# Attention stage of a decoder step: where a step's scores stand on TensorE, and which bank takes the filler behind the transposes

## The reference, cut to what matters

```python
u = rms_norm(x, g_pre) @ w_in          # q: 1024 columns, z: 3 x 1024, gates
l = einsum(q, k) * scale + bias
p = masked_softmax(l, mask, -1)
o = einsum(p, v)
y = sum(gate * o * silu(z), over 3 branches)
x = x + rms_norm(y @ w_out, g_post)
```

## Time and profile before

| | |
|---|---|
| median of 3 runs | 900.47 us (899.14 to 901.45) |
| profiled execution, its own time | 900.51 us |
| its span | 898.7 us |
| TensorE (PE) busy | 867.2 us, 96% of the span |
| VectorE (DVE) busy | 557.3 us, 62% |
| ScalarE (ACT) busy | 452.9 us, 50% |
| GpSimd (POOL) busy | 300.9 us, 33% |
| TensorE in the chain that ended last | 87% of the span |

### The profile page before, as it was taken

One profiled execution on the slowest core, in us unless ns is written; L12 is line 12 of the kernel. 1 busy time (PEld: TensorE's weight loads), 2 busy tenths in 40 slices (PEclk: granted clock), 3 DMA queues, 4 the chain that ended last, 5 costly groups with the idle time before them and its releaser, 6 DMA issues.

```text
span 898.7 us, 16698 instructions
## 1 busy us (share of the span) xinstructions
PE 867.2 (96%) x6202; PEld 755.4 (84%) x6202; DVE 557.3 (62%) x1211; ACT 452.9 (50%) x916; POOL 300.9 (33%) x311
## 2 busy tenths in 40 slices
PE   5999999999999999999999999999999999999996
PEld 4999999956788788889999898999999998786664
DVE  6379999998967772423345555646464655536563
ACT  6466777634643552224446555556464555524231
POOL 2389888888140000012023232333324233400000
PEclk9999999999999999999999999999999999999999
DMA  9355433127269392446323232232232002923521
GB/s 252 97 157 161 120 103 78 54 54 230 66 226 356 139 292 63 111 78 183 95 47 72 49 71 62 58 70 62 58 72 48 24 1 53 274 88 102 184 84 36
DMA packets 158165, 99.52 MB, mean 111 GB/s; under 512 B 97202, under 2 KB 147026, under 8 KB 158005
## 3 DMA queue, kind: packets, MB, share of 16 engines
q1 hardware_dynamic: 143278, 79.30, 33.1%
q0 software_dynamic: 4896, 10.32, 3.2%
q10 hardware_dynamic: 9911, 8.84, 3.0%
HBM read 89.58 MB, written 18.85 MB: 121 GB/s over the span
## 4 chain that ended last, share of the span: by engine, by line
PE 87%; DVE 4%; ACT 3%; issue 3%; ACTq 1%; POOL 1%; DVEq 0%; POOLq 0%
PE psum L2300 8%; PE psum L2301 7%; PE psum L2302 7%; PE psum L1952 6%; PE psum L1953 6%; PE psum L1954 6%; PE psum L2395 6%; PE psum L2030 5%; PE psum L2143 4%; PE psum L2144 4%; PE psum L2145 4%; PE psum L2346 4%; PE psum L2363 3%; PE psum L1933 2%; PE psum L2328 2%
## 5 line engine op out<-in xcount | busy, mean ns | idle before, releaser
L811 ACT ACTIVATE arena<-psum 128x512 f32<-128x512 f32 (+9 forms) x227 | 90.1, 433 | 173.4 <-PE psum L2302 66.4
L2300 PE MATMUL psum<-u_hi,tile_hi 128*128 128x288 f32 x464 | 143.3, 309 | 4.5 <-ACT arena L811 2.1
L790 POOL TENSOR_SCALAR arena<-arena,kept 128x512 f32<-128x512 f32 (+3 forms) x128 | 83.1, 664 | 177.1 <-DVE kept L1789 177.1
L2301 PE MATMUL psum<-u_lo,tile_hi 128*128 128x288 f32 x464 | 137.6, 296 | 0.0
L2302 PE MATMUL psum<-u_hi,tile_lo 128*128 128x288 f32 x464 | 136.4, 294 | 0.0
L1439 DVE SCALAR_TENSOR_TENSOR psum<-arena,psum 128x512 f32<-128x512 f32 x168 | 127.0, 756 | 6.0
L1952 PE MATMUL psum<-h_hi,tile_hi 128*128 128x288 f32 x352 | 104.3, 296 | 0.0
L1953 PE MATMUL psum<-h_lo,tile_hi 128*128 128x288 f32 x352 | 103.8, 295 | 0.0
L1954 PE MATMUL psum<-h_hi,tile_lo 128*128 128x288 f32 x352 | 103.8, 295 | 0.0
L2300 PEld LDWEIGHTS psum<-u_hi,tile_hi 128*128 128x128 f32 x464 | 87.3, 188 | 10.3 <-ACT arena L811 4.0
L1261 ACT ACTIVATE arena<-arena,kept 128x512 f32<-128x512 f32 (+3 forms) x128 | 70.5, 552 | 44.7 <-DVE kept L1755 43.9
(11 more groups left out here) (328 smaller groups left out, 1898.1 us busy)
## 6 DMA issues: line engine op xcount, KB each, us to landing
tile_whole<-in_b_w_in SPq DMA_DIRECT2D x64, 256.0 KB
tile_whole<-in_a_w_in SPq DMA_DIRECT2D x24, 512.0 KB
arena<-in_cmp_w SPq DMA_DIRECT2D x4, 2048.0 KB, 9.8
kvw_whole<-in_w_kv SPq DMA_DIRECT2D x6, 1024.0 KB, 14.1
bias_copies<-bias_line POOLq DMA_DIRECT2D x4, 1280.0 KB, 23.5
arena<-in_x_prompt SPq DMA_DIRECT2D x8, 512.0 KB, 6.5
kvw_whole<-in_a_w_out SPq DMA_DIRECT2D x4, 1024.0 KB, 11.3
arena<-bias_copies SPq DMA_DIRECT2D x16, 256.0 KB, 3.8
```

Source lines behind the costliest of these rows:

```text
L790: pool.tensor_scalar(L, L, rden[:, stat(n) + k:stat(n) + k + 1], gR[:, i, h:h + 1], ALU.mult, ALU.mult).then_inc(S["pn_ready"], 1)
L811: return nc.scalar.activation(out, in_, ACT.Copy, scale=scale)
L2300: pe.matmul(pb(7, HT), w_hi, u_hi[:, k, here], start=(k == 0), stop=False)
L2301: pe.matmul(pb(7, HT), w_hi, u_lo[:, k, here], start=False, stop=False)
```

## The change

TensorE's order in a turn becomes `parts[0]`, `values(n-2)`, `scores(n)`, first transposes, `parts[1]`, second transposes. The halves that stand in `parts[1]` of steps 1, 2 and 4 no longer go to bank 7 but to the scores bank of the same step's first unit (`part_bank`). Such a half waits until VectorE has read that unit (`l_ready`), and the next step's scores wait until the half has been read out. Bank 7's own order (`own`) skips these halves. On ScalarE the read-out of `parts[0]` moves in front of the step's exponentials, and the copy of the first transposes (`pt_copy(n - 1, 0)`) moves behind the second exponential in step 3; in the last round it stood there before.

```diff
+        def in_scores_bank(n):
+            part = tile_parts(n)[1] if n % 5 in (1, 2, 4) else None
+            return part[:2] if part else None
+
+        aside = [in_scores_bank(n) for n in range(5 * KD)]
+        own = [half for half in order if half not in aside]
-        bank_clear = {half: bank_read(before) for before, half in zip(order, order[1:])}
+        bank_clear = {half: bank_read(before) for before, half in zip(own, own[1:])}
...
+        def part_bank(part, n):
+            return steps[n][3][0] % 4 if part[:2] == aside[n] else 7
...
@@ ScalarE
             for n in range(N_STEPS + 1):
+                parts = tile_parts(n)
+                drain(parts[0], n)
                 if n < N_STEPS:
...
                         for j, u in enumerate(us):
...
-                            if j == 1 and n % 5 == 1:
-                                drain(parts[0])
-                            if j == 1 and n >= LAST_PAIR:
+                            if j == 1 and (n >= LAST_PAIR or n % 5 == 3):
                                 pt_copy(n - 1, 0)
-                parts = tile_parts(n)
-                if n % 5 != 1:
-                    drain(parts[0])
-                if 1 <= n < LAST_PAIR or n == N_STEPS:
+                if 1 <= n < LAST_PAIR and n % 5 != 3 or n == N_STEPS:
                     pt_copy(n - 1, 0)
-                drain(parts[1])
+                drain(parts[1], n)
...
@@ TensorE
-            def tile_part(part):
+            def tile_part(part, n):
...
+                b = part_bank(part, n)
...
                     if k == 0:
-                        if (i, hf) in bank_clear:
+                        if b != 7:
+                            pe.wait_ge(S["l_ready"], steps[n][3][0] + 1)
+                        elif (i, hf) in bank_clear:
                             pe.wait_ge(S[bank_clear[i, hf][0]], bank_clear[i, hf][1])
...
             def scores(n):
                 m, br, qs, us = steps[n]
+                if n and aside[n - 1]:
+                    name, count = bank_read(aside[n - 1])
+                    pe.wait_ge(S[name], count)
...
             for n in range(N_STEPS + 2):
+                parts = tile_parts(n)
+                tile_part(parts[0], n)
+                if n >= 2:
+                    values(n - 2)
                 if n < N_STEPS:
                     scores(n)
-                parts = tile_parts(n)
-                tile_part(parts[0])
-                if n >= 2:
-                    values(n - 2)
                 if 1 <= n <= N_STEPS:
                     turns(n - 1, range(2) if steps[n - 1][1] else range(1))
-                tile_part(parts[1])
+                tile_part(parts[1], n)
```

More of the change, by code:

```diff
@@ L1185, in z_copy, with z_copy_half @@
                 copy(szs[:, br, m], hi[:, SEQ - HT:HT]).then_inc(S["zb_ready"], 1)
-            def z_copy_half(n, half):
+            def z_copy_half(n, half, b):
                 m, br = n // NBR, n % NBR
@@ L1191, in z_copy_half @@
                     act.wait_ge(S["y_mul"], 3 * (m - 2) + br + 1)
-                bank = pb(7, HT)
+                bank = pb(b, HT)
                 if half == 0:
@@ L1230, in _, with drain @@
             LAST_PAIR = 5 * (KD - 1) + 2
-            def drain(part):
+            def drain(part, step):
                 if not part or part[2][-1] < KD - 1:
@@ L1237, in drain @@
                 act.wait_ge(S["tile_mm"], half_done[i, hf])
+                b = part_bank(part, step)
                 if kind == "z":
-                    z_copy_half(n, hf)
+                    z_copy_half(n, hf, b)
                 else:
@@ L1242, in drain @@
                     act.wait_ge(S["s_done"], UPM * (n - 1) + 1)
-                    copy(q_full[:, here], pb(7, here.stop - here.start), QSCALE)
-                    copy(q_hi[:, n % 2, here], pb(7, here.stop - here.start), QSCALE).then_inc(S["qk_hi"], 1)
+                    copy(q_full[:, here], pb(b, here.stop - here.start), QSCALE)
+                    copy(q_hi[:, n % 2, here], pb(b, here.stop - here.start), QSCALE).then_inc(S["qk_hi"], 1)
             for n in range(N_STEPS + 1):
+                parts = tile_parts(n)
+                drain(parts[0], n)
                 if n < N_STEPS:
                     m, br, qs, us = steps[n]
-                    parts = tile_parts(n)
                     if br == 0:
@@ L1691, in _, with q_drain @@
             split_lo(6)
-            def q_drain(part):
+            def q_drain(part, step):
                 if not part or part[2][-1] < KD - 1 or stream[part[0]][0] == "z":
@@ L1699, in q_drain @@
                 here = slice(hf * HT, min(hf * HT + HT, SEQ))
-                q_rest(q_lo[:, m % 2, here], pb(7, here.stop - here.start), q_hi[:, m % 2, here])
+                q_rest(q_lo[:, m % 2, here], pb(part_bank(part, step), here.stop - here.start), q_hi[:, m % 2, here])
                 if hf:
-                    q_samples(m, pb(7, HT)[:, SEQ - HT:HT], QSCALE)
+                    q_samples(m, pb(part_bank(part, step), HT)[:, SEQ - HT:HT], QSCALE)
             dve.wait_ge(S["zeroes"], ZEROED["table"])
@@ L1790, in _ @@
                 for part in tile_parts(n):
-                    q_drain(part)
+                    q_drain(part, n)
                 if 1 <= n <= N_STEPS and steps[n - 1][1]:
@@ L2299, in tile_part @@
                     w_hi, w_lo = tile_hi[:, hi_slot(i), k], tile_lo[:, i % TRING, k]
-                    pe.matmul(pb(7, HT), w_hi, u_hi[:, k, here], start=(k == 0), stop=False)
-                    pe.matmul(pb(7, HT), w_hi, u_lo[:, k, here], start=False, stop=False)
-                    ins = pe.matmul(pb(7, HT), w_lo, u_hi[:, k, here], start=False, stop=(k == KD - 1))
+                    pe.matmul(pb(b, HT), w_hi, u_hi[:, k, here], start=(k == 0), stop=False)
+                    pe.matmul(pb(b, HT), w_hi, u_lo[:, k, here], start=False, stop=False)
+                    ins = pe.matmul(pb(b, HT), w_lo, u_hi[:, k, here], start=False, stop=(k == KD - 1))
                     if k == KD - 1:
```

## The result

The changed kernel takes 907.53 us (median of 4, 906.09 to 909.25) against 900.62 us before: ratio 1.0077, 95% interval 1.0064 to 1.0091. It is slower by 0.8%, as forecast; the forecast was 908.5 us. A second measurement, in which the kernel before took 900.37 us, gave 907.0 us and 1.0071 (1.0050 to 1.0092). The profiled execution took 906.09 us, the fastest of the four; its span is 904.3, 5.6 us over the span of before.

The account below looks back on a forecast made before the run. TensorE was taken as the bound, busy 43.1 of 43.7 us a round. Added waits and joints less 11.0 us removed gave +2.2 us, the last round +5.8: 900.5 to 908.5 us, range 900 to 914.5.

Parts of the forecast that it names:

- the three waits of rows 2: Filler waiting for bank 7 in steps 1, 2 and 3; removal forecast to win 3.2, 2.1 and 1.4 us.
- the one at the start: Filler wait of 0.50 us at the very start; 0.56 us taken as won, with the joint.
- Second transposes behind ScalarE's copy: Second transposes wait for bank 4's copy behind exponentials: step 0 adds 5.2 us, step 3 adds 2.9 us.
- Filler waiting for VectorE's read in step 1: Filler in the scores bank waits until VectorE has read unit 0: 0.28 us a round, 2.0 us added.
- Joints: Loss between kinds of matmul: scores behind values add 3.1 us (0 to 7) over four of five steps.
- The joints removed: Some 21 transpose-to-score joints go, 2.3 us; touching filler blocks in step 1 to 2 save 1.4 us.
- Last round: Scores queued behind values join two chains as filler runs out: 5.8 us added (4.8 to 6.8).
- The first idle piece: Last round: TensorE idles some 3 us before V(35), waiting for VectorE's split until S(36) + 5.0 us.
- The forecast's steps of 5.6 to 5.9 us: Last round: spacing of successive score blocks, each waiting for values whose copies stand behind the exponentials.
- the clock, a rival with 3%: Last round: new 3 us idle could bring 1.2 GHz for part of its TensorE work, 911.5 us; 3%.
- the new waits came at full size: Against two rivals: added waits and joints nil, 895.3 us (13%); waits half size, joints nil, 900.3 us (12%).
- the softmax chain was in time for the first transposes: Against the rival that the chain is late there, 1 to 2 us a round, 915 to 922 us; 7%.

## Why the prediction was right, point by point

**Waits removed.** Right: the three waits of rows 2 and the one at the start are gone. With both copies moved as well, a round is 42.49 us, 1.2 under the kernel before.

**Second transposes behind ScalarE's copy.** Right in place and size: 0.70 a round in step 0 (0.74 forecast) and 0.49 in step 3 (I took 0.42 between bounds of 0.34 and 0.49). Moving the copy alone, with nothing else changed, takes away 0.58 of the first and all of the second.

**Filler waiting for VectorE's read in step 1.** 0.30 against 0.28.

**Joints.** The terms that were mis-sized, on both sides. I charged 0.11 for scores behind values in four steps, 3.1 us (the upper bound there, 0.22 x 28, is 6.2 and not 7). It is 0 behind the value products of steps 1 to 4, and 0.11 behind the three products of step 0; the first transposes behind step 0's scores start 0.12 later (0.94 instead of 0.82) and get 0.05 of it back, and the eight in step 2 take 0.06 more: 0.2 a round in all, where I had 0.44. The joints removed gave more than I took. Four second transposes take 0.38 in front of filler, where they took 0.53 in front of scores, twice a round; the pairs take 0.14 (552.82 to 552.96), where they took 0.22 and 0.31: 0.55 a round, where I had 0.33. So the rounds came out 0.1 us shorter each, not 0.3 longer, and the stage up to the last round 1.5 us shorter instead of 2.2 us longer. All of the 1.5 is won in the first round, with its start (1.6 us); from there to S(36) both kernels take the same to 0.1 us, where my terms set them some 3 us apart. Of the two halves of the Trainium skill's rule (TensorE: Matmul & The Clock Gate, the step-by-step of part 2), a load into the background buffer fits the joint of 0 behind the value products of steps 1 to 4, and a load held back where row groups conflict fits the 0.11 behind step 0's; what decides between them no run here shows.

**Last round.** Right in mechanism, a little small: 6.7 us against 5.8. The first idle piece ends at S(36) + 4.94 (5.0 forecast), and the order of scores and values alone gives all but 0.1 of the 6.7 back. The forecast's steps of 5.6 to 5.9 us are 6.05 to 6.4. That the sum came near has a part of luck. Its terms for a step (3.36 + 0.5 + 0.8 to 1.0 + 0.3 + 0.4 + 0.1) add up to 5.5 to 5.7, not 5.6 to 5.9; at the upper clock such steps took 5.53 (761.02 to 766.55 with TensorE kept busy over the first gap) and 6.08 (768.89 to 774.97 in the changed kernel). And the clock, a rival with 3% and a price of 3 us, did fall to 1.2 GHz behind the idle piece and made values and scores there 1.2 us slower. Without that the last round would be some 5.5 us longer than before, an estimate from these rows, so the mechanism that I had forecast carries most of the loss and the clock a fifth of it. Two traces of the changed kernel show one fall and two falls in the last round, with last rounds of 27.6 and 28.3 us; together with the start of the stage, which moves by up to 4 us from trace to trace, this is wide enough for the spread of 3 to 5 us between executions. Why the start moves stays open.

The two errors, -3.7 us up to the last round and +0.9 in it, partly cancel, and that is luck too: with the start of the stage 0.4 us later they lead from 908.5 to 906.1, the time of the profiled execution; the median of 907.5 lies nearer to the forecast than this account. The sign that I had named, a round of 44.0 us, didn't come: it is 43.6. The other rivals fell: the new waits came at full size, and the softmax chain was in time for the first transposes in every full round.

## What to carry to other kernels

Where work is reordered to lengthen the cover of one chain, ask which chain loses that cover, and look at the rounds without filler first: one edit of order that wins 1.5 us over the first 35 steps lost 6.7 us in the last round, and a condition on the step number gives it back. When an instruction becomes the critical release of a bank, look at what stands in front of it in its engine's queue: two copies that stood behind exponentials cost 1.2 us a round, of which 1.1 came back when they were moved, one of them to a place where ScalarE had been idle. A kernel as full as this (43.1 of 43.7 us) is read best by the distance between blocks on the bounding engine, which gave waits right to 0.1 us; joints between kinds of matmul could not be carried over from another pair.

## What the runs showed of the hardware that was not expected

- A joint between two kinds of matmul depends on both: scores behind transposes 0.11 us, behind 64-column value products 0, behind full-width ones 0.11.
- A granted clock of 0.50 in a last round that ran at 1.00 before: it fell behind 3.1 us in which PE did nothing, and a 512-column product's record grew from 0.47 to 0.71 us.
- In the last round the clock fell in all six traces of kernels that have values in front of scores there, and in none of the five others. In three of the six it fell a second time, behind a gap of 1.4 or 1.9 us, and where the gap of 3.1 us was filled with transposes it fell behind one of 1.9 us alone; in the four others the same gap of 1.9 us passed at a clock of 1.00.
